# A third row pair of gate and up as seven block products of sums, with a new order of units, in a one-core SwiGLU trunk kernel

## What is computed

```python
    hf = rms_norm(x, norm_ffn)                       # 256 x 2048
    gate, up = jnp.split(hf @ w_gu, 2, axis=-1)      # w_gu: 2048 x 11264, so gate and up are 256 x 5632
    return x + (jax.nn.silu(gate) * up) @ w_down     # w_down: 5632 x 2048
```

## Time and profile before

| what | value |
|---|---|
| median of 3 runs | 1102.86 us (1102.61 to 1103.05) |
| the profiled execution | 1103.19 us, its span 1101.5 us |
| busy, share of span | PE 99%, DVE 78%, ACT 53%, POOL 4% |
| bytes moved | 215.31 MB, mean 195 GB/s |
| groups 1 to 10 of gate and up | about 430 to 864 us of the span |

### The profile page before, as it was taken

The page is one execution under the profiler, slowest core; times in us unless marked ns, Lnnn a source line. Parts: engine busy times, 40 slices in busy tenths (PEclk is TensorE's granted clock), DMA queues, the critical chain, the costliest instruction groups (busy, mean ns, idle before and its releaser), DMA issues.

```text
span 1101.5 us, 13909 instructions
## 1 busy us (share of the span) xinstructions
PE 1090.1 (99%) x5101; PEld 906.9 (82%) x5101; DVE 864.0 (78%) x1061; ACT 580.9 (53%) x705; POOL 40.6 (4%) x68
## 2 busy tenths in 40 slices
PE   8999999999999999999999999999999999999997
PEld 7897889888888888888888888888888888888885
DVE  5556866688756557988988888889888899899896
ACT  5655545555445444545545545546455556546553
POOL 2600000000010000000000000000000000000000
PEclk9999999999999999999999999999999999999999
DMA  8765646465546575656657557566565766666663
GB/s 285 217 197 168 189 128 183 154 172 153 190 176 223 178 267 171 211 171 215 202 158 230 167 174 241 175 192 210 170 212 194 282 203 216 199 200 213 195 226 116
DMA packets 110941, 215.31 MB, mean 195 GB/s; under 512 B 6956, under 2 KB 11632, under 8 KB 110000
## 3 DMA queue, kind: packets, MB, share of 16 engines
q1 hardware_dynamic: 108976, 205.36, 59.2%
q0 software_dynamic: 1632, 8.96, 2.2%
q10 hardware_dynamic: 288, 0.39, 0.1%
HBM read 210.49 MB, written 4.19 MB: 195 GB/s over the span
## 4 chain that ended last, share of the span: by engine, by line
PE 96%; DVE 2%; DMA 1%; issue 1%; SPq 0%; ACT 0%; POOLq 0%; POOL 0%; ACTq 0%; DVEq 0%
PE acc L1693 11%; PE acc L1694 11%; PE acc L1695 11%; PE acc L1413 11%; PE acc L1414 11%; PE acc L1415 11%; PE acc L1758 5%; PE acc L1759 5%; PE acc L1760 5%; PE mx L1405 2%; PE mx L1693 2%; PE mx L1694 2%; PE mx L1695 2%; PE mx L1758 1%; PE mx L1759 1%; PE mx L1760 1%
## 5 line engine op out<-in xcount | busy, mean ns | idle before, releaser
L759 DVE TENSOR_TENSOR w_lo<-raw,w_hi 128x1024 fp32r<-128x1024 f32 (+2 forms) x144 | 166.7, 1169 | 117.8 <-ACT w_hi L454 117.0
L454 ACT ACTIVATE w_hi<-raw 128x1024 fp32r<-128x1024 f32 (+2 forms) x143 | 143.4, 1013 | 135.0 <-PE acc L1415 132.7
L648 ACT ACTIVATE w_hi<-raw 128x1024 fp32r<-128x1024 f32 (+1 forms) x160 | 158.4, 1005 | 94.4 <-PE acc L1695 86.7
L1693 PE MATMUL acc<-w_hi,hT_hi 128*128 128x512 f32 x520 | 203.3, 391 | 0.0
L1179 DVE TENSOR_TENSOR w_lo<-raw,w_hi 128x1024 fp32r<-128x1024 f32 (+1 forms) x160 | 180.5, 1154 | 29.0 <-ACT w_hi L648 27.2
L1694 PE MATMUL acc<-w_lo,hT_hi 128*128 128x512 f32 x520 | 202.4, 389 | 0.0
L1695 PE MATMUL acc<-w_hi,hT_lo 128*128 128x512 f32 x520 | 202.3, 389 | 0.0
L1413 PE MATMUL acc<-w_hi,hT_hi 128*128 128x512 f32 (+2 forms) x416 | 157.7, 379 | 0.0
L1415 PE MATMUL acc<-w_hi,hT_lo 128*128 128x512 f32 (+2 forms) x416 | 155.5, 374 | 0.0
L1414 PE MATMUL acc<-w_lo,hT_hi 128*128 128x512 f32 (+2 forms) x416 | 155.5, 374 | 0.0
L1695 PEld LDWEIGHTS acc<-w_hi,hT_lo 128*128 128x128 f32 x520 | 97.6, 188 | 20.5
(11 more groups left out here) (299 smaller groups left out, 1553.3 us busy)
## 6 DMA issues: line engine op xcount, KB each, us to landing
raw<-in_w_gu SPq DMA_DIRECT2D x176, 512.0 KB, 4.2
raw<-in_w_down SPq DMA_DIRECT2D x88, 512.0 KB, 4.5
raw<-in_w_in SPq DMA_DIRECT2D x79, 512.0 KB, 3.9
raw<-in_w_out SPq DMA_DIRECT2D x32, 512.0 KB, 4.3
raw<-in_w_in SPq DMA_DIRECT2D x8, 272.0 KB, 2.8
raw<-in_w_in SPq DMA_DIRECT2D x8, 264.0 KB, 2.8
x<-in_x POOLq DMA_DIRECT2D x2, 1024.0 KB, 8.0
x_kept<-x POOLq DMA_DIRECT2D x2, 1024.0 KB, 6.1
```

Source lines behind the costliest of these rows:

```text
L648: act.activation(w_hi[:, v % R, c0:UC * GW], raw[:, i % R, c0:UC * GW], ACT.Copy).then_inc(hi_ready, 1)
L759: dve.tensor_tensor(w_lo[:, slot, 0:UC * width], raw[:, slot, 0:UC * width], w_hi[:, slot, 0:UC * width].bitcast(F32), ALU.subtract).then_ ...
L1693: pe.matmul(o, a[0], w[0], start=first, stop=False)
```

## The change

Three row pairs in place of two run as sevens in groups 1 to 10, and the order is: gate 3, 4, 5, seven 0, gate 6, 7, seven 1, up 3, 4, seven 2, up 5, 6, 7. That is 22 slots (v0 to v21) and 10 x 12 + 3 x 21 = 183 matmuls. 22 is no multiple of 4, so the rings are turned by two slots in every other group (`ring`), and the loops over groups take two groups in one pass (`lin`). The two units of each seven now lie in `raw[3]` and `raw[0]`, so the first weight sum reads its second operand with a step of -3 tiles. The activation sums of the third pair are made once, in `third_summands`. The gate is one `Silu` on ACT in place of a tanh on ACT and `gated` on DVE. ACT makes the copy L1117 that DVE made. `act_sums` stands behind the weight sums of seven 0, `fold_gate` ahead of the low half of up 6, and `fold_up` behind up 7.

```diff
+FF_SUMMED = 3
+FF_ORDER = [("gate", 3, 0, 0), ("gate", 4, 1, 1), ("gate", 5, 2, 2), ("seven", 0, 3, 3), ("gate", 6, 5, 7), ("gate", 7, 6, 8),
+            ("seven", 1, 7, 9), ("up", 3, 9, 13), ("up", 4, 10, 14), ("seven", 2, 11, 15)] \
+    + [("up", k, 8 + k, 14 + k) for k in range(5, UPG)]
+FF_SLOTS = 22
...
+SEVEN_END = {k: v + 4 for kind, k, _i, v in FF_ORDER if kind == "seven"}
...
+def ring(j, v):
+    return (v + 2 * ((j[1] - 1) % 2)) % R
...
+                freed = FF_SLOT_OF[12] - FF_SLOTS if i == 0 and j > 1 else FF_SLOT_OF[i - R]
+                sp.wait_ge(lo_ready, j * FF_SLOTS + (FF_BASE + freed + 1))
```

```diff
-                    act.activation(gate_s[:, b, :], acc[:, b, :], ACT.Tanh, scale=half_rs_h[:, b:b + 1])\
-                       .then_inc(sem("gate_tanh"), 1)
+                    act.activation(gate_s[:, b, :], acc[:, b, :], ACT.Silu, scale=rs_h[:, b:b + 1])\
+                       .then_inc(sem("gate_used"), 1)
...
+                if kept is not None:
+                    act.activation(actT_lo32[:, bass.ds(kept, 1), P:2 * P].rearrange("p c t -> p (c t)"), mx[:, 0, P:2 * P],
+                                   ACT.Copy).then_inc(sem("a21_kept"), 1)
...
+                act.wait_ge(sem("ff_sums_made"), 8)
+                act.activation(third_hi.rearrange("p c t -> p (c t)"), third_32.rearrange("p c t -> p (c t)"), ACT.Copy)\
+                   .then_inc(sem("ff_hi_ready"), 1)
...
-                    if kind == "up" and k == 4:
-                        act.wait_ge(unit_used, j * FF_SLOTS + (FF_BASE + 12))
-                        act.wait_ge(lo_ready, j * FF_SLOTS + (FF_BASE + 13))
+                    if kind == "up" and k == 7:
+                        act.wait_ge(unit_used, lin(j, FF_SLOTS, FF_BASE + SEVEN_END[2]))
+                        act.wait_ge(lo_ready, lin(j, FF_SLOTS, FF_BASE + SEVEN_END[2]))
                         act.activation(ff_sum[:, 0, 0, :], mx[:, 2, :], ACT.Copy).then_inc(sem("p1_kept"), 1)
...
-                    if kind == "up" and k == 6:
-                        act.wait_ge(sem("gate_folded"), j * 2)
-                        gate_tanh(j * FF_SLOTS + (FF_BASE + 14), j * 2)
+                act.wait_ge(sem("gate_folded"), lin(j, 2))
+                gate_silu(lin(j, FF_SLOTS, FF_BASE + SEVEN_END[2]), lin(j, 2))
```

DVE:

```diff
+                upper = raw[:, a:a + 2, 0:GW] if b > a else raw[:, a::b - a, 0:GW]
+                dve.tensor_tensor(ff_sum[:, 0, :, :], raw[:, b, :].rearrange("p (k n) -> p k n", k=UC), upper,
+                                  ALU.subtract).then_inc(sem("ff_w_sums"), 1)
...
             def fold_gate(j):
 
-                dve.wait_ge(unit_used, j * FF_SLOTS + (FF_BASE + 14))
-                dve.wait_ge(sem("p1_kept"), j)
+                dve.wait_ge(unit_used, lin(j, FF_SLOTS, FF_BASE + SEVEN_END[2]))
+                dve.wait_ge(sem("p1_kept"), lin(j, 1))
...
                     if kind == "seven":
                         ff_weight_sums(j, i, k, opening)
+                        if k == 0 and summed:
+                            act_sums(j, bass.ds(lin(j, 1, -1), 1))
+                        elif k == 0:
+                            act_low(lin(j, 1), lin(j, 4, -4))
+                    if kind == "up" and k == 6:
+                        fold_gate(j)
                     ff_low(j, i, v)
...
-                    if kind == "up":
-                        if k == 5:
-                            fold_gate(j)
-                        if k == 6:
-                            fold_up(j)
-                        if k == 7:
-                            gated(j * 2)
+                    if kind == "up" and k == 7:
+                        fold_up(j)
```

More of the change, by code:

```diff
@@ L58, with lin @@
 U_DN = U_FF + NG_FF * 2 * UPG
-FF_ORDER = [("gate", 2, 0, 0), ("gate", 3, 1, 1), ("gate", 4, 2, 2), ("gate", 5, 3, 3), ("seven", 0, 4, 4),
-            ("gate", 6, 6, 8), ("gate", 7, 7, 9), ("seven", 1, 8, 10)] + [("up", k, 8 + k, 12 + k) for k in range(2, UPG)]
-FF_SLOTS = 20
-FF_BASE = U_FF + 2 * UPG - FF_SLOTS
-FF_SLOT_OF = [-4, -3, -2, -1] + [v + d for kind, _k, _i, v in FF_ORDER for d in ((0, 1) if kind == "seven" else (0,))]
+FF_SUMMED = 3
[3 more added lines that the diff above has]
+FF_SLOTS = 22
+FF_BASE = U_FF + 2 * UPG - FF_SLOTS
+SEVEN_END = {k: v + 4 for kind, k, _i, v in FF_ORDER if kind == "seven"}
+FF_SLOT_OF = {i - R: i - R for i in range(R)}
+for _kind, _k, _i, _v in FF_ORDER:
+    FF_SLOT_OF[_i] = _v
+    if _kind == "seven":
+        FF_SLOT_OF[_i + 1] = _v + 1
+def lin(j, m, c=0):
+    p, o = j
+    return o * m + c if p is None else p * (2 * m) + (o * m + c)
+def ring(j, v):
+    return (v + 2 * ((j[1] - 1) % 2)) % R
 V_DN = FF_BASE + FF_SLOTS * NG_FF
@@ L614, in _, with gate_silu @@
                         out_high(n)
-            def gate_tanh(used, gates_read=None):
+            def gate_silu(used, gates_read=None):
                 act.wait_ge(unit_used, used)
@@ L1065, in _ @@
                         out_low(n)
[L1067 to L1072, removed]
             def up_part(b):
@@ L1144, in ff_summands, with third_summands @@
                 dve.tensor_tensor(s4, a12_, s2, ALU.subtract).then_inc(sem("ff_sums_made"), 1)
+            def third_summands():
+                full = actT_lo32[:, FC - 2:FC, :]
+                a11, a21_, a12_, a22_ = (full[:, c, b * P:(b + 1) * P] for c in range(2) for b in range(NB))
+                s1, s3, s2, s4 = (third_32[:, i // 2, (i % 2) * P:(i % 2 + 1) * P] for i in range(4))
+                step(dve.tensor_tensor(full.rearrange("p c t -> p (c t)"),
+                                       hT_hi[:, 4:6, :].rearrange("p c t -> p (c t)").bitcast(F32),
+                                       hT_lo[:, 4:6, :].rearrange("p c t -> p (c t)").bitcast(F32), ALU.add))
+                settle()
+                dve.tensor_tensor(s1, a21_, a22_, ALU.add).then_inc(sem("ff_sums_made"), 1)
+                dve.tensor_tensor(s3, a11, a21_, ALU.subtract).then_inc(sem("ff_sums_made"), 1)
+                dve.wait_ge(sem("ff_sums_made"), 5)
+                dve.tensor_tensor(s2, s1, a11, ALU.subtract).then_inc(sem("ff_sums_made"), 1)
+                dve.wait_ge(sem("ff_sums_made"), 7)
+                dve.tensor_tensor(s4, a12_, s2, ALU.subtract).then_inc(sem("ff_sums_made"), 1)
             def ff_summands_low():
@@ L1165, in first_gate_up @@
                         dve.wait_ge(sem("rs_h_ready"), 1)
[L1166 to L1171, removed]
                     if k == 13:
                         ff_summands()
+                        third_summands()
@@ L1188, in ff_weight_sums @@
             def ff_weight_sums(j, i, k, opening=False):
[L1190 to L1193, removed]
-                    dve.wait_ge(lo_ready, j * FF_SLOTS + (FF_BASE + 8))
+                a, b = i % R, (i + 1) % R
+                for n in (i, i + 1):
+                    dve.wait_ge(loaded[n % R], lin(j, 16 * 2 * UPG // R, 16 * ((U_FF + n) // R + 1)))
@@ L1743, in gate_up @@
                     if v == 0:
-                        act_transposed(j * 2, None if opening else j - 1)
+                        act_transposed(lin(j, 2), None if opening else lin(j, 1, -1))
             first_gate_up()
-            gate_up(1, True)
-            with pe.Fori(2, NG_FF) as j:
-                gate_up(j)
+            gate_up((None, 1), True)
+            with pe.Fori(1, NG_FF // 2) as p:
+                gate_up((p, 0))
+                gate_up((p, 1))
+            gate_up((None, NG_FF - 1))
             opened = set()
```

149 lines of the change are left out of this document (82 added, 67 removed).

## The result

The changed kernel takes 1117.65 us (median of 4 runs, 1117.21 to 1119.88) against 1102.87 us before (median of 4 runs as well): a ratio of 1.0138, 95% interval 1.0122 to 1.0154. It is slower by 14.8 us, though it issues 30 matmuls fewer. The forecast was 1119.0.

What follows compares the result with a forecast made beforehand. PE, busy 99% of the span, was taken as the bound. Matmuls -6.8, the wait at up 6 +19.9 and the chain to seven 0 +3 gave +16.1 us, so 1119.0 us, range 1113 to 1125.

Steps and rivals of the forecast that it cites:

- Part 1: PE's matmuls: 3 fewer in each of ten groups, 6.8 us off PE's work.
- Part 2: At up 6, PE waits for the fold and low half: 1.99 us per group with restart, 19.9 us in all.
- Part 3: DVE's queue from the end of seven 2 to the next seven 0: +0.3 us per group, +3 in all (-2 to +8).
- Part 4: Other DVE and ACT work, loads, Silu's table and the negative step: no cost; DVE fits with 40.1 us of 42.6.
- A: Rival: the fold at the end of seven 2 is covered and only the matmul saving remains, 1096 us; chance 0.06.
- B: Rival: PE waits at up 6 for less than reckoned, 1 us or less, about 1103 to 1111 us; chance 0.06.
- C: Rival: DVE becomes the bound and seven 0 waits 0.8 to 1.4 us per group, 1124 to 1130 us; chance 0.12.
- D: Rival: the clock falls for the 12 matmuls behind each wait, 27 us more, 1146 us; chance 0.03.

Runs made afterwards that it cites:

- both edits: Changed kernel with fold_gate moved behind the low half of up 6 and ACT's copy of P1 run before seven 2 ends: 1096.23 us, ratio 0.9935.
- more work in the chain: Changed kernel with two more DVE operations of 512 columns (1.2 us) ahead of fold_up, behind the low half of up 7: 1127.02 us, ratio 1.0228.
- extra work ahead of the fold: Changed kernel with two more DVE operations of 512 columns (1.2 us) ahead of fold_gate: 1116.53 us, ratio 1.0128.
- early copy: Changed kernel with ACT's copy of P1 waiting only for earlier slots of seven 2, so it runs before the seven ends: 1109.47 us, ratio 1.0054.

## Why the prediction was right

**Part 1, the matmuls.** -6.8 us. The kernel with both edits bears it out, though not cleanly: the 6.9 us between 1103.1 and 1096.2 are 7.7 less in the groups and 1.0 more at the down projection, so that the total comes so near to 6.8 is in part luck.

**Part 2, the fold.** Put at 1.99 us per group, measured 2.09, of it 0.11 for the restart in both. The other 1.97 stand against 1.88: the copy took 0.60 in place of 0.58, and the fold started 0.10 behind its end (645.27 to 645.37) where I had 0.04 for every handover. The four operations and the low half took what they took before. Moving the fold and moving the copy took off what they were said to.

**Part 3, the chain to seven 0.** This is the term that was wrong. I put it at +0.3 us per group, and it was -0.2: the small loss there went. From the end of seven 2 to the end of the first low half of seven 0 it took 662.24 + 1.22 - 644.63 = 18.83 us in place of 19.3, and PE wanted it at 19.21 in place of 18.98. The low half of the activations and their sums were to take 2.5 us and took 2.01, from DVE's first row below to its last:

```profile
660.23 0.95 DVE L1137 TENSOR_TENSOR actT_lo<-mx,actT_hi 128x768 f32 x1
661.10 0.28 DVE L1142 TENSOR_TENSOR actT_lo<-mx,actT_hi 128x128 f32 x1
661.29 0.28 DVE L1148 TENSOR_TENSOR s<-mx,actT_lo 128x128 f32 x1
...
662.24 1.81 DVE L1223 TENSOR_TENSOR w_lo<-raw,w_hi 128x1024 fp32r<-128x1024 f32 x2
```

I had kept the 1.37 us from the start of the low half to the start of the copy (609.34 to 610.71), with the gap ahead of that copy in it, where the two operations now take 1.06 (660.23 to 661.29); the small operations behind them take 0.15 less too. The lower bound that I gave for part 3, a chain half a microsecond shorter, is what came. The down projection, which I had counted as one of the ten, was the only place that waited, at its entry and its first seven, with 1.5 us more than before. Together +3 was forecast and -0.2 came.

**Part 4.** Two rows of the changed kernel, the weight sum with the negative step (groups by line) and ACT's wait for loads (waits of the group loops: us in total, times, longest):

```profile
L1245 DVE TENSOR_TENSOR ff_sum<-raw 128x1024 f32<-128x1024 f32 x30 | 36.6, 1219 | 0.0
```

```profile
ACT w_hi L675 <- DMA raw<-in_w_gu: 14.8, 8, 3.1
```

The step costs nothing. The loads are late for ACT at times, by up to 3.1 us, which I had not expected; none of it reached PE.

**The sum.** Forecast +16.1 on the profiled execution, measured +14.5 between the spans. Part 3 was 3.2 too high, part 2 was 1.0 too low, and the clock's 1.6 was left out. The transposes (-0.4) and the earlier start of group 1 (-0.5) stand in no part of the forecast, and 0.1 is left. The errors partly cancel, so the closeness of the total says less than the rows do.

**The rivals.** A (1096 us) and B are refuted by ten equal gaps; A's time is what the kernel gives with both edits. C did not come: seven 0 had 0.3 us to spare, and the kernel with both edits keeps PE busy with DVE at 94%. D was put aside too quickly: no row settled it, and the clock did fall, behind one of ten waits here and four of ten with more work in the chain, for 1.6 us each time and not for a whole unit behind each wait. The Trainium skill (TensorE: Matmul & The Clock Gate, HAM oscillation — how this bites in real kernels) tells of a kernel that fell back to the low clock in every tile because TensorE waited for data. These runs agree in that the clock, while PE had work, fell only behind such waits; they differ in that it fell behind 5 of 30 waits of the same 1.82 us, and only 0.9 to 1.6 us after PE had taken up work again.

## What to carry to other kernels

When engines hand each other work through rings, ask of every blocking step in an engine's program what it stands in front of, and how much finished work its consumer holds at that moment; the sum of busy times tells nothing of it. Here the same four operations cost 2.1 us per group, or 1.4, or nothing, by their place and by the wait of one copy ahead of them. Before adding or removing work on an engine, find whether the place is inside the chain that ends at the bound engine's next need: 1.2 us per group cost nothing on one side of a wait, and about 1 us per group on the other (0.9 in the changed kernel, falls of the clock included, and 1.1 in the one with both edits).

## What the runs showed of the hardware that was not expected

Behind waits of TensorE of 1.82 us that are equal to 0.01 us, the granted clock fell to the lower level in some and not in others: in the profiled runs behind one of ten in the changed kernel, none of ten with extra work ahead of the fold, four of ten with extra work behind it. So something other than the length of the wait decides, and what it is was not tested. Behind the ten waits of 1.1 us it did not fall in the profiled run of the early copy, nor in that of the kernel before with its fold moved early. Each fall came 0.9 to 1.6 us after PE had taken up work again, lasted about 3.4 us and cost 1.6 us. It may be why the changed kernel's runs reach from 1117.21 to 1119.88: the slowest has the lowest mean granted clock, 0.994 against 0.996 and 0.997. One fall, 3.4 us at half the clock, takes 0.0015 off that mean, so by this estimate two more falls, 3.2 us, would explain it. A two-source VectorE operation in float32 whose operand steps backwards over tiles took the same 1.22 us as one that steps forwards. And a first matmul of 512 columns behind a wait is followed by one interval of 0.33 or 0.34 us in place of 0.227, for waits from 0.1 to 1.8 us; behind the waits at the transposes, of 128 columns, the interval grew only from 0.11 to 0.16.
